# Expert lookup of 256 tokens: the last 32 tokens leave the first expert table too

## What is computed

```python
q = (xb @ w_q).reshape(t, PEER_HEADS, 2, PEER_HALF)
s = jnp.einsum('thpd,hpkd->thpk', q, sub_keys)
top_s, top_i = lax.top_k(s, K)
cand_s = top_s[:, :, 0, :, None] + top_s[:, :, 1, None, :]
cand_i = top_i[:, :, 0, :, None] * PEER_N_KEYS + top_i[:, :, 1, None, :]
best_s, best_pos = lax.top_k(cand_s.reshape(t, PEER_HEADS, K * K), K)
idx = jnp.take_along_axis(cand_i.reshape(t, PEER_HEADS, K * K), best_pos, axis=-1)
gate = jax.nn.softmax(best_s, axis=-1)
h = jax.nn.gelu(jnp.einsum('thkd,td->thk', u_table[idx], xb), approximate=False)
return jnp.einsum('thk,thkd->td', gate * h, v_table[idx])
```

## Time and profile before

| | |
|---|---|
| median of 3 runs | 1385.64 (1385.4 to 1386.0) |
| profiled execution | 1384.31 |
| its span (first to last instruction) | 1382.5 |
| mean granted TensorE clock | 0.992 |
| busy: TensorE | 1341.2 (97%) |
| busy: weight loads of TensorE | 1234.6 (89%) |
| busy: VectorE | 900.8 (65%) |
| busy: ScalarE | 846.3 (61%) |
| busy: GpSimd | 917.4 (66%) |
| bytes read from HBM | 267.81 MB |
| u table | about 651 to 1045.5 |
| v table | 1045.5 to about 1367 |

### The profile page before, as it was taken

One profiled execution on the slowest core, in us unless ns is written; L12 is line 12 of the kernel. 1 busy time (PEld: TensorE's weight loads), 2 busy tenths in 40 slices (PEclk: granted clock), 3 DMA queues, 4 the chain that ended last, 5 costly groups with the idle time before them and its releaser, 6 DMA issues.

```text
span 1382.5 us, 28792 instructions
## 1 busy us (share of the span) xinstructions
PE 1341.2 (97%) x9918; PEld 1234.6 (89%) x9918; DVE 900.8 (65%) x1908; ACT 846.3 (61%) x1444; POOL 917.4 (66%) x463
## 2 busy tenths in 40 slices
PE   7999999999999999989999999999998998999996
PEld 6878888888898777879999999999998998999996
DVE  3784884024764664444999101999994987888885
ACT  5475775436865656456666755888885454555553
POOL 7875899886675523876988878777776443576410
PEclk9999999999999999999999999999999999999999
DMA  5633556555443411654556556566667899899981
GB/s 204 207 134 123 179 200 200 193 188 173 135 168 123 137 63 62 228 177 159 185 190 193 187 166 217 183 204 198 200 203 275 314 340 352 313 335 327 334 301 58
DMA packets 99695, 280.92 MB, mean 203 GB/s; under 512 B 28200, under 2 KB 28584, under 8 KB 99368
## 3 DMA queue, kind: packets, MB, share of 16 engines
q1 hardware_dynamic: 79504, 234.62, 50.8%
q0 software_dynamic: 8448, 25.20, 4.8%
q10 hardware_dynamic: 11672, 20.17, 4.2%
HBM read 267.81 MB, written 12.06 MB: 202 GB/s over the span
## 4 chain that ended last, share of the span: by engine, by line
PE 35%; POOL 11%; issue 8%; DMA 5%; DVE 4%; ACT 1%; POOLq 0%; DVEq 0%; SPq 0%; ACTq 0%
PE PS L1186 16%; POOL WL L462 10%; PE PS L1809 10%; PE PS L1810 4%; DMA RAW<-weights 3%; PE PS L1749 2%; DMA stage<-gates_rest 1%; DVE WL L2609 1%; ACT WH L1092 0%; DVE sparse_y L2626 0%; POOL h_s L526 0%; PE PS L1526 0%; DVE XS L2425 0%; POOL group_sum L541 0%; DVE hot_j L2554 0%
## 5 line engine op out<-in xcount | busy, mean ns | idle before, releaser
L462 POOL TENSOR_TENSOR WL<-RAW,WH 128x1024 fp32r<-128x1024 f32 x306 | 739.5, 2429 | 264.1 <-ACT WH L563 179.1
L1186 PE MATMUL PS<-XHL,WH 128*128 128x256 f32 x2528 | 460.1, 284 | 3.0 <-DVE XHL L1911 1.5
L1186 PEld LDWEIGHTS PS<-XHL,WH 128*128 128x128 f32 x2528 | 394.0, 192 | 6.6 <-issue 3.4
L1186 PE MATMUL PS<-XHL,WL 128*128 128x256 f32 x1264 | 357.6, 283 | 0.0
L1809 PE MATMUL PS<-CHL,WH 128*128 128x416 f32 x1024 | 310.8, 369 | 9.7 <-DVE CHL L2583 9.7
L1810 PE MATMUL PS<-CHL,WL 128*128 128x208 f32 x1024 | 264.7, 259 | 0.0
L563 ACT CAST WH<-RAW 128x1024 fp32r<-128x1024 f32 x184 | 191.3, 1047 | 106.1 <-PE PS L1186 96.1
L1186 PEld LDWEIGHTS PS<-XHL,WL 128*128 128x128 f32 x1264 | 242.5, 192 | 0.0
L1092 ACT CAST WH<-RAW 128x1024 fp32r<-128x1024 f32 x128 | 134.6, 1051 | 150.6 <-DMA RAW<-weights 85.4
L1809 PEld LDWEIGHTS PS<-CHL,WH 128*128 128x128 f32 x1024 | 193.1, 189 | 12.8 <-DVE CHL L2583 10.5
L1810 PEld LDWEIGHTS PS<-CHL,WL 128*128 128x128 f32 x1024 | 196.4, 192 | 0.0
(11 more groups left out here) (430 smaller groups left out, 2061.6 us busy)
## 6 DMA issues: line engine op xcount, KB each, us to landing
RAW<-weights SPq DMA_DIRECT2D x438, 512.0 KB, 3.6
gates_rest<-stage ACTq DMA_DIRECT2D x26, 256.0 KB, 2.2
stage<-gates_rest ACTq DMA_DIRECT2D x7, 512.0 KB, 8.8
stage_odd<-gates_rest ACTq DMA_DIRECT2D x6, 512.0 KB, 6.8
hidden<-HS SPq DMA_DIRECT2D x29, 96.0 KB, 3.6
H<-x SPq DMA_DIRECT2D x2, 512.0 KB, 4.7
LG<-rows ACTq DMA_DIRECT2D x2, 512.0 KB, 6.0
LB<-rows ACTq DMA_DIRECT2D x2, 512.0 KB, 9.8
```

Source lines behind the costliest of these rows:

```text
L462: nc.gpsimd.tensor_tensor(WL[:, slot, :], RAW[:, slot, :], plain(WH[:, slot, :]), ALU.subtract).then_inc(w_lo, 1)
L1186: last = mm(dst, a, b, start=start and k == 0, stop=stop and k == len(pairs) - 1)
```

## The change

`SETS` is cut to its second entry: 32 sparse tokens instead of 48, so 224 dense ones instead of 208. The sparse tokens leave the u table as well:

- The u steps take 224 columns instead of 256, the v steps 448 and 224 instead of 416 and 208. `HS` holds dense tokens alone; the room behind it takes `x_late`, `sparse_y` and three buffers `gathered`.
- GpSimd gathers 64 rows in one sequence: 32 of the u table (from a copy of the table in row order, `u_rows`), then 32 of v. The gathers of hidden values and the stores to `hidden` are gone.
- VectorE's `dot` multiplies a gathered u row by the token's own row (`x_late`, four transfers more of ScalarE) and sums it into `dots`. 10 dots lie beside u items 54 to 65, 22 beside v items 4 to 55; ScalarE applies one Gelu at v item 61; 32 `add_row` lie at v items 64 to 120.
- For u items 54 to 65 (`W0` to `W1`) VectorE makes the low halves, and GpSimd issues 13 gathers instead.
- The lists are exchanged after u item 51 (`IJG_AT` = 13), gates start at item 68 (`HOT_AT` = 17), and there are 14 groups of them (56 items) and 14 parked blocks. `chosen` takes 4 transfers instead of 12.
- The transfers for the last norm go from v item 40 to 44; the first of the two `sparse_back` goes behind the last `back`.

```diff
-SETS = ((80, 16), (96, 32))
+SETS = ((96, 32),)
...
-IJG_AT = NK // 8 - 2
+IJG_AT = 13
...
+W0, W1 = 54, 4 * HOT_AT - 2
+EARLY = 10
+DOT_AT = [W0 + 1 + k * (W1 - W0) // EARLY for k in range(EARLY)] + [
+    4 + k * 54 // (STEPS - EARLY) for k in range(STEPS - EARLY)]
+ADD_AT = [64 + k * 58 // STEPS for k in range(STEPS)]
+ROWS = 3 if len(SETS) == 1 else 4
...
-    "h_stored": ("vec_landed", 16),
+    "late_hidden": ("sgp_out", 4),
...
-SELF_STORED = NK // 4 - 3
...
-        HS = at("HS", [P, NK, S], F32, A0)
+        HS = at("HS", [P, NK, TD], F32, A0)
...
+        LATE = A0 + NK * TD * 4
+        x_late = [at(f"x_late{k}", [P, D], F32, LATE + 4 * D * k) for k in range(len(SETS))]
+        sparse_y = [at(f"sparse_y{k}", [P, D], F32, LATE + 4 * D * k) for k in range(len(SETS))]
+        gathered = at("gathered", [P, ROWS, D], F32, LATE + 4 * D * len(SETS))
...
+            full = (N_ITEMS // RING) * RING
+            with sp.Fori(1, N_ITEMS // RING) as i:
...
-            with sp.Fori(0, SELF_STORED) as k:
-                four_items(k * RING + store_from * RING)
-                sp.wait_ge(sem("u_bank_free"), 2 * k + 2)
-                sp.dma_start(h_dram[bass.ds(4 * k, 4)].rearrange("j p t -> p j t"),
-                             HS[:, bass.ds(4 * k, 4), TD:S]).then_inc(sem("h_stored"), 16)
...
+            U0, V0 = FIRST["u"], FIRST["v_table"]
+            assert (U0 + W0) % RING == 0 and (U0 + W1) % RING == 0
+            with pool.Fori(keys + 1, (U0 + W0) // RING) as i:
+                for slot in range(RING):
+                    split_low(i * RING + slot, slot)
+            value_rows = weights.rearrange("n p d -> (n p) d")
+            def gather(n):
+                if n >= ROWS:
+                    pool.wait_ge(sem("row_added"), late_at("row_added", n - ROWS + 1))
+                table, k = (u_rows, n) if n < STEPS else (value_rows, n - STEPS)
+                nc.gpsimd.indirect_dma_start(
+                    out=gathered[:, n % ROWS, :], out_offset=None, in_=table,
+                    in_offset=bass.IndirectOffsetOnAxis(ap=chosen[:, n // STEPS, k:k + 1], axis=0)).then_inc(
+                        sem(f"row_landed{n % ROWS}"), 16)
+            pool.wait_ge(sem("chosen_landed"), late_at("chosen_landed", 16 * 2 * PICKS))
+            for n in range(EARLY + ROWS):
+                gather(n)
+            pool.wait_ge(w_lo, U0 + W1)
+            with pool.Fori((U0 + W1) // RING, full) as i:
...
-            pool.wait_ge(sem("chosen_landed"), late_at("chosen_landed", 16 * PICKS))
             pool.wait_ge(w_used, V0)
-            for k in range(ROWS):
-                gather_row(k)
...
-            pool.wait_ge(sem("h_stored"), late_at("h_stored", 16 * (SELF_STORED + 1)))
-            for k in range(2 * BATCH):
-                gather_hidden(k)
-            for k in range(STEPS - ROWS):
-                gather_row(k + ROWS)
-                if k == FEW:
-                    pool.wait_ge(w_used, V0 + 42)
+            for n in range(EARLY + ROWS, 2 * STEPS):
+                gather(n)
+                if n == STEPS + ROWS:
+                    pool.wait_ge(w_used, V0 + 50)
                     nc.gpsimd.memset(dense_y[:, :, TD:S], 0.0).then_inc(sem("units_ready"), 1)
-                if k + 2 * BATCH < STEPS:
-                    gather_hidden(k + 2 * BATCH)
...
-                A(HS[:, bass.ds(4 * i + 2 * half, 2), :], PS[:, half, :].rearrange("p (j s) -> p j s", j=2),
+                A(HS[:, bass.ds(4 * i + 2 * half, 2), :], PS[:, half, :].rearrange("p (j s) -> p j s", j=2)[:, :, 0:TD],
                   ACT.Gelu).then_inc(sem("u_bank_free"), 1)
...
-            with act.Fori(0, IJG_AT - 2) as i:
+            with act.Fori(0, IJG_AT - 1) as i:
                 u_body(i)
 
             act.wait_ge(sem("bv_ready"), late_at("bv_ready", 1))
             A(be[:, :, :, :], be[:, :, :, :], ACT.Exp).then_inc(sem("bexp_ready"), 1)
-            with act.Fori(IJG_AT - 2, IJG_AT) as i:
+            with act.Fori(IJG_AT - 1, IJG_AT) as i:
...
+            act.wait_ge(sem("x2_stored"), 16)
+            for s, (first, n) in enumerate(SETS):
+                for g in range(P // n):
+                    act.dma_start(x_late[s][n * g:n * g + n, :], x2_dram[first:first + n, D:2 * D]).then_inc(
+                        sem("chosen_landed"), 16)
...
-            act.wait_ge(sem("u_bank_free"), NK // 2)
-            act.dma_start(h_dram[4 * SELF_STORED:NK].rearrange("j p t -> p j t"),
-                          HS[:, 4 * SELF_STORED:NK, TD:S]).then_inc(sem("h_stored"), 16)
...
-                if j == 40:
-                    act.wait_ge(w_used, V0 + 32)
+                if j == 61:
+                    act.wait_ge(sem("row_added"), late_at("row_added", STEPS))
+                    A(h_s[:, :], dots[:, :], ACT.Gelu).then_inc(sem("late_hidden"), 1)
+                if j == 44:
+                    act.wait_ge(w_used, V0 + 40)
...
-                        last = split([(wh, XH[:, k, :]), (wh, XL[:, k, :]), (wl, XH[:, k, :])],
-                                     PS[:, c // 2, (c % 2) * S:(c % 2 + 1) * S], k == 0, k == KC - 1)
+                        last = split([(wh, XH[:, k, 0:TD]), (wh, XL[:, k, 0:TD]), (wl, XH[:, k, 0:TD])],
+                                     PS[:, c // 2, (c % 2) * S:(c % 2) * S + TD], k == 0, k == KC - 1)
...
-                wait("row_added", late_at("row_added", STEPS))
+                wait("row_added", late_at("row_added", 2 * STEPS))
...
-                if ch == KC - 2:
-                    sparse_back(0)
+            sparse_back(0)
...
-            V.tensor_scalar(found_late[late, 0, :], expert[late, :], float(FIRST["v_table"] * P), None, ALU.add)
-            V.tensor_scalar(found_late[late, 1, :], expert[late, :], float(TS), eps_c[late, 2:3], ALU.mult, ALU.add)
+            V.tensor_scalar(found_late[late, 0, :], expert[late, :], 0.0, None, ALU.add)
+            V.tensor_scalar(found_late[late, 1, :], expert[late, :], float(FIRST["v_table"] * P), None, ALU.add)
...
+            def dot(k):
+                wait(f"row_landed{k % ROWS}", 16 * (k // ROWS + 1))
+                V.scalar_tensor_tensor(gathered[:, k % ROWS, :], gathered[:, k % ROWS, :], 1.0, x_late[set_of(k)][:, :],
+                                       ALU.mult, ALU.mult, accum_out=dots[:, k:k + 1]).then_inc(sem("row_added"), 1)
+            def add_row(k):
+                n, y = STEPS + k, sparse_y[set_of(k)]
+                if k == 0:
+                    wait("late_hidden", late_at("late_hidden", 1))
+                    link(V.tensor_tensor(h_s[:, :], h_s[:, :], gate_s, ALU.mult))
+                wait(f"row_landed{n % ROWS}", 16 * (n // ROWS + 1))
+                wait("row_added", late_at("row_added", n))
+                if k in (0, SETS[0][1]):
+                    V.tensor_scalar(y[:, :], gathered[:, n % ROWS, :], h_s[:, k:k + 1], None, ALU.mult).then_inc(
+                        sem("row_added"), 1)
+                else:
+                    V.scalar_tensor_tensor(y[:, :], gathered[:, n % ROWS, :], h_s[:, k:k + 1], y[:, :],
+                                           ALU.mult, ALU.add).then_inc(sem("row_added"), 1)
+            U0 = FIRST["u"]
+            dve.wait_ge(w_lo, U0 + W0)
+            for j in range(W0, W1):
+                slot = (U0 + j) % RING
+                dve.wait_ge(w_hi, U0 + j + 1)
+                dve.wait_ge(w_used, U0 + j + 1 - RING)
+                V.tensor_tensor(WL[:, slot, :], RAW[:, slot, :], plain(WH[:, slot, :]), ALU.subtract).then_inc(w_lo, 1)
+                for k in range(EARLY):
+                    if DOT_AT[k] == j + 1:
+                        dot(k)
...
+            wait("chosen_landed", late_at("chosen_landed", 16 * 2 * PICKS))
...
-            def add_row(k):
-                if k % BATCH == 0:
-                    wait(f"h_landed{k // BATCH % 2}", 16 * BATCH * (k // BATCH // 2 + 1))
-                    batch = slice(k, k + BATCH)
-                    link(V.tensor_tensor(h_s[:, batch], h_s[:, batch], gate_s[:, batch], ALU.mult))
-                wait(f"row_landed{k % ROWS}", 16 * (k // ROWS + 1))
-                wait("row_added", late_at("row_added", k))
-                s = 0 if k < SETS[0][1] else 1
-                if k == SETS[0][1]:
-                    dve.wait_ge(w_used, V0 + 48)
-                if k in (0, SETS[0][1]):
-                    V.tensor_scalar(sparse_y[s][:, :], rows_v[:, k % ROWS, :], h_s[:, k:k + 1], None, ALU.mult).then_inc(
-                        sem("row_added"), 1)
-                else:
-                    V.scalar_tensor_tensor(sparse_y[s][:, :], rows_v[:, k % ROWS, :], h_s[:, k:k + 1],
-                                           sparse_y[s][:, :], ALU.mult, ALU.add).then_inc(sem("row_added"), 1)
...
+                for k in range(EARLY, STEPS):
+                    if DOT_AT[k] == j:
+                        dot(k)
                 for k in range(STEPS):
-                    if MAC_AT[k] == j:
+                    if ADD_AT[k] == j:
...
```

(1 more changed line is left out.)

45 lines of the change are left out of this document (7 added, 38 removed).

## The result

| | before | after |
|---|---|---|
| median | 1385.52 (1384.35 to 1386.0, 4 runs) | 1375.38 (1373.34 to 1377.16, 4 runs) |
| profiled execution | 1384.31 | 1376.38 |
| its span | 1382.5 | 1374.6 |

The ratio is 0.993, with a 95% interval of 0.9916 to 0.9943, so 10.1 faster in the medians. The two profiled executions differ by 7.9; the sum of the prediction was made against the first of them. Forecast were 3.1. The direction and the range were right, the gain was some three times as large.

What follows compares the result with a forecast made beforehand. TensorE's steps were taken to bound both table loops while the other engines keep up. The terms -22.8 + 6.8 + 7.7 + 13.7 - 7.3 + 0.5 - 1.7 gave -3.1, a median of 1382.5; 8-in-10 range 1374 to 1396.

Steps and rivals of the forecast that it cites:

- 1. Plain u items: u table without gates: 76 items at 2.88 become 72 of 24 steps at 0.1135, -22.8.
- rival of the lower floor: Step price: 0.111 for 224 columns, as the 128-column steps show; 1373 in all, chance 0.12.
- 2. Gated items: u items with gates: 52 at 3.39 become 56 at 3.27, TensorE and VectorE both needing 3.20, +6.8.
- 3. Exchange: Exchange of the index lists in the u table: TensorE stands twice, 8.5 lost for 0.79 before, +7.7.
- 4. v pairs: v loop: 128 items of 8 pairs, each pair 0.0133 dearer by its wide half alone, +13.7.
- 5. Start of the v table: VectorE's wait for gathered hidden values, TensorE's stand of 5.60 and 1.7 of slow clock go, -7.3.
- 6. Waits in the v table's middle: TensorE's 4.1 of waits near the last norm's transfers stay, at 346 GB/s asked for 343, +0.5.
- rival of a DMA-bound first half: v loop's first half: 49.3 MB at 345 GB/s take 142.8 for TensorE's 135.6; about 1390, chance 0.12.
- 7. End: After the last pair: row sums come behind tile 0's norm, one set instead of two, -1.7.
- rows that hold the splits: Exchange: late gathered rows hold VectorE's in-order splits and so stop TensorE, 9.8 more; 1392, chance 0.17.

Runs made afterwards that it cites:

- ladder: Changed kernel with u items at 256 to 128 columns a step and v items at six pairs of widths, columns left out or added; 1373.04 in one run.
- sets48: Changed kernel with 48 sparse tokens instead of 32 in both tables and 14 early dots instead of 10; 1379.06 in one run.
- norm_at_44: Kernel before, with only the transfers for the last norm issued at v item 44 instead of 40; 0.9986 of before.
- spread6: Changed kernel, quotient chain behind the low half of u item 57, only 6 dots beside u items (59 to 64), 26 beside v items; 1375.58, 0.9916 of before.
- after_again: The changed kernel itself, run again on one chip beside three variants; 1373.67, 0.9921 of before.
- u256: Changed kernel with u steps of 256 columns again; 1393.65, 1.0069 of before.
- quot_later: Changed kernel with VectorE's quotient chain moved behind the low half of u item 57; 1376.37, 0.9943 of before.
- spread6_norm_68: spread6 with the last norm's transfers issued at v items 68, 74, 80 and 86 instead of all at 44; 1366.58, 0.9856 of before.
- both_later: Changed kernel with quotients behind the low half of u item 57 and the ten dots at items 57 to 65; 1373.69, 0.9916 of before.
- rows_from_12: Kernel before, with its first row of v added at v item 12 instead of 8; 0.9986 of before.
- no_h_gathers: Kernel before, with the 48 gathers of single hidden values replaced by constant fills; 0.997 of before.
- dots_later: Changed kernel with the ten dots moved to u items 57 to 65; 1374.99, 0.9929 of before.

## Why the prediction was right, and where its size was off

The signs of six of its seven terms and its range held, and four of them came within 0.4. The gain was 7.9 for 3.1 since terms 1 and 6 gave more than was put down for them. Point by point, by the numbers of its sum, between the two profiled executions:

1. Plain u items: forecast -22.8, measured 72 x 2.68 for 76 x 2.88, **-25.9**. The mis-sized term is the step of 224 columns: 0.1117, not 0.1135. The rival of the lower floor (0.111, 1373) had it right. The ladder settles it: the floor is flat from 128 to 224 columns and 240 nearly lie on it. The Trainium skill (TensorE: Matmul & The Clock Gate, LDWEIGHTS) would have 0.1067 here; no step of 128 to 224 columns in the ladder came under 0.1117, so the measurement decides against that figure.
2. Gated items: +6.8, measured 56 x 3.275, **+7.1**. The number was right, the reason in part: with steps of 0.1117 TensorE needs 3.16, not 3.20, so the two engines are not at one pace. VectorE's 3.20 holds the item up, and 0.07 is lost beside it.
3. Exchange: +7.7, measured 10.2 for 0.8, **+9.3**. The path was right, and its times came a little sooner than forecast: the copies 5.1 behind TensorE's last restart (5.6), item 54's split finished 10.0 behind (10.4), TensorE's stand 4.41 (5.0), the first landing 4.4 behind the gather's start (5.8). The second stand came one item later, since the second row took 7.9. What was mis-sized is the half clock: 0.4 in the forecast, but there were two stretches of 3.4 that cost 1.7 each; the stands were shorter than forecast, 6.4 for 8.1.
4. v pairs: +13.7, measured 0.3134 for 0.3004, **+13.3**.
5. Start of the v table: **-7.3** as forecast. The reason given, that the wait for gathered hidden values goes, was half of it. The runs show that the wait would have passed to the parked gates, had the gathers not gone as well.
6. Waits in the v table's middle: +0.5, measured 1.4 for 4.1, **-2.7**. The step that failed is that an equal demand (346 GB/s for 343) would keep the waits, with 345 to 350 taken as the limit. It was no limit: 409 between 1150 and 1160 in the changed kernel and in the one before, 379 over 140 in sets48. The 345 was the average of a full and an emptier stretch. What took the waits away is open: norm_at_44, with the same later item, kept 4.6, while the v waits of the changed kernel and of its versions with 448 and 224 columns, other than spread6, are 2.0 at most. The rival of a DMA-bound first half rested on the ceiling too and was wrong for the kernel as it is. Yet its mechanism was at work just beyond: spread6 fell into it.
7. End: **-1.6**, for -1.7.

These sum to -7.8, for -7.9 between the executions. So two terms, 1 and 6, hold -6.3 more than forecast, and 2 to 4 give 1.5 back. The other 2 in the medians are not in these two profiles. The profiled execution of the changed kernel was one of its slower ones; after_again, at 1374.65, came to its u table 1.7 sooner, so part of it lies ahead of the tables.

Of the rivals, rows that hold the splits (1392) had its landings at 11.3 first and 8.1 after; the trace has a median of 8.0, but 4.4 for the first, and where a dot waits behind a landing TensorE does stand. It is there with 2.0 instead of 9.8. As for the Trainium skill's rule (SBUF — State Buffer, "DVE blocks DMA") that spoke against the change, the trace neither bears it out nor refutes it: gathers take GpSimd 0.94 to 1.90 here, 1.68 in the median, as before. Of the three that take 0.94, two lie where VectorE is idle and one where it is busy all through. No run here separates what part of a landing time comes from that.

Settled by runs are the floor (ladder, u256) but for the two odd v pairs, the two stands of the exchange and their cause (quot_later to spread6), and the norm's transfers (spread6_norm_68). Not shown is which transfers, beside the gathers of single values, crowd the start of the v table, what took the waits in its middle away, and why 6.8 at the lower clock followed one stand and none another.

## What to carry to other kernels

Price a matmul's width by a ladder, not by one neighbour: between a floor and the columns there is a corner (here near 240 columns). Over it a column is worth 0.42 ns (0.120 for 256 columns, 0.227 for 512), under it nothing. Before an in-order engine takes over work that another waits for, write down when each of its inputs lands; put the dependent work two turns behind that, and count the turns of its buffers. And when a repair gives nothing, compare the arrival times of later stages: here 9 were won at one place and spent at a burst of transfers some 120 items later. And before an average rate is taken for a limit, cut its stretch into shorter ones: 345 GB/s over 20 was 409 over the first 10.

## What the runs showed of the hardware that was not expected

- The floor of a step with new stationary data is flat: 0.1117 at 128, 160, 192, 208 and 224 columns, 0.112 at 240, 0.120 at 256, while a wide step costs more with its columns (0.188 to 0.191 at 416, 0.2017 at 448). A v pair of 448 and 208 columns was dearer than one of 448 and 224 (0.3158 for 0.3134).
- After stands of equal length the granted clock may fall or not: 3.3, 2.5 and 1.5 within 26 in both_later, and 3.05 ahead of item 6 in rows_from_12, had no stretch at 1.2 GHz behind them; 2.8 in no_h_gathers and the second 3.05 in rows_from_12 had 3.4, and 2.9 in norm_at_44 and 4.25 in spread6 had 6.8. The first stand of the exchange, 4.41 in three runs, had 3.4 in the changed kernel and 6.8 in after_again and dots_later.
- The core's DMA moved 379 GB/s for 140 with TensorE never idle, and 409 over a stretch of 10: in the changed kernel with TensorE never idle, in the kernel before with TensorE idle for 1.1 of it.
